# A streaming transformer step: the last output tile by token half, and the next norm and scaling beside its second half

## The chip, the cores and the metric

One core of one Trainium2 chip runs the whole step as one program. The metric is the device time of one execution, in microseconds (us); less is better.

## The reference

A two-layer trunk with a prompt of 512 tokens and a sample of 32, model width 1024. Each layer is FFN, mixer, FFN, each with a modulated norm before it and a gated, normed residual behind it:

```python
def modulated_pre(x, g, mods, j):
    return rms_norm(x, g) * (1.0 + mods[:, 3 * j + 1, None]) + mods[:, 3 * j, None]
def gated_post(x, o, g, mods, j, coef):
    return x + coef * mods[:, 3 * j + 2, None] * rms_norm(o, g)
mods = silu(c) @ ada_w[l] + ada_b[l]          # 9 x 1024 numbers for the prompt, 9 x 1024 for the sample
x = gated_post(x, swiglu(modulated_pre(x, ..., 0), w1, w3, w2), norm_post[l, 0], mods, 0, 0.5)
x = gated_post(x, mixer(modulated_pre(x, ..., 1)), norm_post[l, 1], mods, 1, 1.0)
x = gated_post(x, swiglu(modulated_pre(x, ..., 2), w1, w3, w2), norm_post[l, 2], mods, 2, 0.5)
```

The mixer is latent attention beside retention; the change doesn't touch its inside.

## The kernel before

All activations lie with features on the 128 partitions and the T = 544 tokens along the row: x is 8 tiles of 128x544 (KD = 8). TensorE (PE) multiplies in two halves of HT = 272 tokens, one PSUM bank each. Every weight and every activation is split into a high and a low part (w_hi, w_lo, h_hi, h_lo), and one product is three: hi x hi, hi x lo, lo x hi (tile3, L654). ScalarE (ACT) casts a weight chunk to w_hi (high, L1107), GpSimd (POOL) subtracts for w_lo (low, L537). There are two slots of weight chunks, so a chunk is cast only when the chunk before the last is used up (w_used), and SyncE loads the next into raw when the low part is done.

An FFN is an up phase (22 feature tiles) and an out phase of 8 output tiles with 22 k-tiles each (out_tiles, L746); the mixer's out phase has 8 k-tiles. j counts the three parts of a layer: 0 and 2 are the FFNs, 1 the mixer. During an FFN's out phase VectorE (DVE) computes the modulations (ada_group, L1443): 48 tiles with two dots each (L1454) in a layer's first FFN, 24 in its second. The dots read the conditioning vector spread over PSUM banks 4 to 7.

A "turn" is what stands between the last product of an out phase and the next stage. It is written out by hand, in the order of each engine's queue:

- After an output tile, ACT squares it (L1212) and scales it to o_buf (L1221, L1223), POOL adds the squares (L547).
- PE waits until the squares are added and, for j = 0 and 2, until all dots are done (ada_done, L772), since it now uses banks 4 and 5. It sums the squares of each token (token_sums, L675, L678), ACT takes the root (L1125), DVE the inverse (L1482), PE spreads it over the partitions (spread, L682, L686, L687).
- DVE turns over (L1477): for each of the 8 tiles o times the inverse (L1491), then x plus that (L1494); three of the eight adds go to POOL (add_odd, L556). ACT scales each new x tile to h_hi (L1136), DVE makes h_lo (L1523).
- PE's first_tiles (L690) does the first two weight chunks (w = 0, 1) in a special order: first all products with h_hi (L701, L703), each k-tile as it comes, for both chunks and both halves; then chunk 0 with h_lo (L711), and after each of its k-tiles the sum of the squares of that x tile over the partitions (pre_sum, L718, L671), which ACT makes in two buffers in turn (L1144); then chunk 1 with h_lo. ACT's root (L1121) and DVE's inverse (L1527) of these sums are needed only to read out the finished tiles.
- The third weight chunk is cast when chunk 0 is used up (w_used at its last h_lo product).

There are five such turns, after (layer 0, j = 0), (0, 1), (0, 2), (1, 0) and (1, 1), and after (1, 2) only the x update and the stores of y. At the start, (0, 0) has first_tiles without a turn before it.

## Time and profile before

| | |
|---|---|
| median of 3 runs | 2378.63 us (2377.84 to 2381.17) |
| profiled execution | 2378.93 us |
| its span | 2377.1 us |
| granted TensorE clock, mean | 0.98 |
| PE, DVE, ACT, POOL busy | 97%, 52%, 34%, 37% |

### The profile page before, as it was taken

To read this page: it belongs to the slowest core of one execution; us is meant where nothing else is said; L and a number is where in the kernel's file an instruction comes from. 1 tells how busy PE (TensorE), PEld (TensorE's weight loads), DVE (VectorE), ACT (ScalarE), POOL (GpSimd) and SP (SyncE) were. 2 spreads that over 40 slices of the span, in tenths; PEclk is the share of its full clock that TensorE was granted. 3 is DMA by queue.
4 is the path that set the end of the run, shared out by engine and by line. 5 is a ranking of instruction groups with operands and counts; after the bars stand their busy time and mean duration, and the time that the engine had idled before them with its cause. 6 is when DMAs were issued, how large, how long until landed. Compare 5 with 4: busy or idle time off the path is not lost.

```text
span 2377.1 us, 44378 instructions
## 1 busy us (share of the span) xinstructions
PE 2311.3 (97%) x17736; PEld 2195.5 (92%) x17736; DVE 1234.7 (52%) x2091; ACT 808.5 (34%) x1332; POOL 878.9 (37%) x382
## 2 busy tenths in 40 slices
PE   8999999999999999999999999999999999999997
PEld 7999999899558999999999999998994699999997
DVE  5333379867471433338143333996856524333561
ACT  3322232333454423332243333224343543333321
POOL 1333444334113344434434434443431153333353
PEclk8999999999999999999999999999999999999999
DMA  6222268322211122236312223782231022222552
GB/s 232 89 88 88 83 236 295 141 89 80 73 36 54 63 84 84 88 129 241 107 60 84 88 88 121 272 271 100 80 111 51 1 71 71 88 88 88 190 200 73
DMA packets 73240, 272.05 MB, mean 114 GB/s; under 512 B 8960, under 2 KB 10368, under 8 KB 72640
## 3 DMA queue, kind: packets, MB, share of 16 engines
q1 hardware_dynamic: 73152, 270.84, 33.1%
q8 instruction: 60, 0.98, 0.2%
q14 instruction: 28, 0.23, 0.0%
HBM read 267.36 MB, written 3.45 MB: 114 GB/s over the span
## 4 chain that ended last, share of the span: by engine, by line
PE 70%; issue 16%; DVE 6%; POOL 3%; DMA 2%; ACT 2%; SPq 1%; DVEq 0%; POOLq 0%; ACTq 0%
PE ps L661 19%; PE ps L665 19%; PE ps L662 19%; POOL w_lo L540 3%; DVE wide_v L1454 2%; PE ps L671 2%; DMA ada_w<-in_ada 2%; PE ps L701 1%; PE ps L703 1%; PE ps L1025 1%; PE ps L910 1%; PE ps L1048 1%; PE ps L992 1%; PE ps L998 1%; DMA ada_first<-in_ada 1%
## 5 line engine op out<-in xcount | busy, mean ns | idle before, releaser
L540 POOL TENSOR_TENSOR w_lo<-raw,w_hi 128x1024 fp32r<-128x1024 f32 (+1 forms) x304 | 785.6, 2584 | 1349.9 <-ACT w_hi L1118 956.9
L661 PE MATMUL ps<-h_hi,w_hi 128*128 128x272 f32 x3296 | 887.4, 289 | 7.7 <-POOL w_lo L540 7.7
L662 PE MATMUL ps<-h_lo,w_hi 128*128 128x272 f32 x3296 | 889.2, 287 | 0.0
L665 PE MATMUL ps<-h_hi,w_lo 128*128 128x272 f32 x3296 | 685.7, 289 | 0.0
L661 PEld LDWEIGHTS ps<-h_hi,w_hi 128*128 128x128 f32 x3296 | 619.1, 188 | 10.5 <-POOL w_lo L540 10.3
L662 PEld LDWEIGHTS ps<-h_lo,w_hi 128*128 128x128 f32 x3296 | 620.9, 188 | 0.2
L1118 ACT CAST w_hi<-raw 128x1024 fp32r<-128x1024 f32 (+1 forms) x236 | 268.6, 1138 | 837.1 <-PE ps L665 753.1
L665 PEld LDWEIGHTS ps<-h_hi,w_lo 128*128 128x128 f32 x3296 | 519.2, 188 | 0.0
L661 PE MATMUL ps<-u_hi,w_hi 128*128 128x272 f32 x1408 | 381.2, 288 | 3.8 <-POOL w_lo L540 3.8
L662 PE MATMUL ps<-u_lo,w_hi 128*128 128x272 f32 x1408 | 380.2, 288 | 0.0
L1454 DVE CUSTOM_DVE_ANT_0 wide_v<-ada_w,ps 128x1024 bf16<-128x1024 f32 x288 | 332.2, 1218 | 47.5 <-DMA ada_w<-in_ada 29.4
L1541 DVE TENSOR_TENSOR wide_v<-ps,rinv 128x544 f32<-128x544 f32 x88 | 63.7, 724 | 439.5 <-PE ps L665 439.5
L665 PE MATMUL ps<-u_hi,w_lo 128*128 128x272 f32 x1408 | 292.0, 288 | 0.0
L661 PEld LDWEIGHTS ps<-u_hi,w_hi 128*128 128x128 f32 x1408 | 265.3, 188 | 4.7 <-POOL w_lo L540 4.7
L662 PEld LDWEIGHTS ps<-u_lo,w_hi 128*128 128x128 f32 x1408 | 264.8, 188 | 0.0
L1546 DVE SCALAR_TENSOR_TENSOR wide_v<-wide_v,wide_s 128x512 f32<-128x512 f32 (+1 forms) x176 | 193.9, 1140 | 104.7 <-ACT wide_s L1184 104.7
L665 PEld LDWEIGHTS ps<-u_hi,w_lo 128*128 128x128 f32 x1408 | 220.0, 188 | 0.0
L1187 ACT CAST u_hi<-wide_v 128x544 f32 (+1 forms) x88 | 56.9, 647 | 213.7 <-DVE wide_v L1546 213.7
L1111 ACT CAST w_hi<-raw 128x1024 fp32r<-128x1024 f32 x68 | 71.0, 1044 | 138.6 <-PE ps L665 88.2
L1482 DVE RECIPROCAL tok_inv<-tok_root 128x5 f32<-128x5 f32 x6 | 1.1, 189 | 205.2 <-ACT tok_root L1125 205.2
L1551 DVE TENSOR_TENSOR u_lo<-wide_v,u_hi 128x544 f32 x88 | 63.9, 726 | 80.0 <-ACT u_hi L1187 80.0
L1184 ACT ACTIVATE wide_s<-wide_s 128x512 f32<-128x512 f32 (+1 forms) x176 | 81.9, 513 | 5.6 <-DVE wide_s L1538 5.6
(256 smaller groups left out, 2382.3 us busy)
## 6 DMA issues: line engine op xcount, KB each, us to landing
raw<-in_w_up SPq DMA_DIRECT2D x176, 512.0 KB, 3.4
ada_w<-in_ada SPq DMA_DIRECT2D x144, 512.0 KB, 5.0
raw<-in_w_dn SPq DMA_DIRECT2D x64, 704.0 KB, 5.3
raw<-in_w_mix SPq DMA_DIRECT2D x64, 512.0 KB, 3.5
ada_first<-in_ada SPq DMA_DIRECT2D x10, 512.0 KB, 8.0
decay<-in_decay SPq DMA_DIRECT2D x2, 2048.0 KB, 9.8
ada_first<-in_ada_first SPq DMA_DIRECT2D x6, 512.0 KB, 11.4
x<-in_x SPq DMA_DIRECT2D x4, 544.0 KB, 16.4
```

The lines of the kernel that those rows point to most:

```text
L540: pool.tensor_tensor(w_lo[:, slot, 0:width], raw[:, slot, 0:width], w_hi[:, slot, 0:width].bitcast(F32), ALU.subtract).then_inc(lo_done.se ...
L661: pe.matmul(ps[:, bank + t, 0:width[t]], wh, hi[:, n], start=start, stop=False)
L662: pe.matmul(ps[:, bank + t, 0:width[t]], wh, lo[:, n], start=False, stop=False)
L665: last = pe.matmul(ps[:, bank + t, 0:width[t]], wl, hi[:, n], start=False, stop=stop)
L1111: nc.scalar.copy(w_hi[:, slot, 0:width], raw[:, slot, 0:width]).then_inc(hi_done.sem, 1)
L1118: nc.scalar.copy(w_hi[:, k, 0:width], raw[:, k, 0:width]).then_inc(hi_done.sem, 1)
L1184: nc.scalar.activation(wide_s[:, f, at], wide_s[:, f, at], ACT.Silu, bias=wide_s[:, f, T + 2 * v:T + 2 * v + 1]).then_inc(up_silu.sem, 1)
L1187: nc.scalar.copy(u_hi[:, bass.ds(i * 2 + f, 1), :].rearrange("p a n -> p (a n)"), tmp_v[:, f, :]).then_inc(up_hi.sem, 1)
L1454: v_.tensor_tensor_reduce(junk[v], ada_w[:, t, :], c_psum(v), 1.0, 0.0, ALU.mult, ALU.add, acc[:, v, t:t + 1]).then_inc(ada_done.sem, 1)
L1541: v_.tensor_tensor(halves(tmp_v[:, f, :]), pair(4 * f + 2), halves(rinv[:, :]), ALU.mult)
L1546: v_.scalar_tensor_tensor(out=wide_v[:, f, at], in0=wide_v[:, f, at], scalar=wide_v[:, f, T + 2 * v:T + 2 * v + 1], in1=wide_s[:, f, at], ...
L1551: v_.tensor_tensor(u_lo[:, at, :].rearrange("p a n -> p (a n)"), tmp_v[:, f, :], u_hi[:, at, :].rearrange("p a n -> p (a n)").bitcast(F32) ...
```

## The change

- The last output tile goes by token half (last_tile on PE and ACT): all its k-tiles for tokens 0 to 271, then all again for 272 to 543. Inside the second half, after four k-tiles, PE makes the first half's token sums (half_sums, with the wait for all dots), and after eleven the spread; the mixer's tile has only eight k-tiles and spreads behind the last.
- DVE updates x by half, each with 8 multiplications and 8 additions of 272 columns, all on DVE. Its inverse for the second half stands before the seventh tile of the first half.
- ACT scales x to h_hi by half (one instruction for the first half, two for the second, which ends with the 32 sample tokens).
- The second half's token sums and spread stand in first_tiles, which now goes chunk 0 with h_hi of the first half, chunk 1 with the same, then both with the second half; then the h_lo pass as before.
- ACT squares the x tiles between the second half's scalings. Tiles 0 to 3 are added by POOL (add_x_squares) and summed by PE once (early_sum); tiles 4 to 7 are summed by PE one by one, after every second k-tile of chunk 0.
- DVE's h_lo comes behind all x updates, first half first.
- In the last layer's second FFN the last 16 modulation tiles, whose results nothing used, aren't loaded or computed.

The diff cut to its core; removed lines are in the functions above.

```diff
...
+TOK_AT = [0, P, HT - P]
 TOK = len(TOK_AT)
...
+SUM_AT = HT + NS
+N_EARLY = 4
...
                 for t in range(ADA_RING, per - ahead):
                     ada_tile(0, t)
+                last = s == 1 and l == DEPTH - 1
                 with sp.Fori(1, 4 - s) as i:
...
+                    down(i, ada=not last)
                 if s == 1:
...
+            def add_x_squares(l, j, m):
+                pool.wait_ge(x_sq.sem, x_sq.at(l, j * KD + m + 1))
+                if m == 1:
+                    pool.tensor_tensor(squares[:, :], tmp_s[:, 0, :], tmp_s[:, 1, :], ALU.add).then_inc(sq_added.sem, 2)
+                else:
+                    pool.wait_ge(sq_added.sem, sq_added.at(l, j * SQ + m))
+                    pool.tensor_tensor(squares[:, :], squares[:, :], tmp_s[:, m % 2, :], ALU.add)\
+                        .then_inc(sq_added.sem, 1)
...
+                for m in range(1, N_EARLY):
+                    add_x_squares(l, j, m)
...
+            def half_sums(l, j, t):
+                if t == 0:
+                    pe.wait_ge(sq_added.sem, sq_added.at(l, (j + 1) * SQ))
+                    if j != 1:
+                        pe.wait_ge(ada_done.sem, ada_done.at(
+                            l, 2 * (ADA_A if j == 0 else ADA_A + (ADA_B if l < DEPTH - 1 else KD))))
+                token_sums(squares[:, :], t, True, False)
+                if t:
+                    pe.wait_ge(out_sq.sem, out_sq.at(l, (j + 1) * KD))
+                else:
+                    pe.wait_ge(half_sq.sem, half_sq.at(l, j + 1))
+                token_sums(tmp_s[:, 1, :], t, False, True).then_inc(sums.sem, 1)
+            def spread(l, j, t):
+                pe.wait_ge(inverted.sem, inverted.at(l, 3 * j + 2 + t))
+                for b in range(2):
+                    c = t * TOK + b
+                    pe.transpose(ps[:, 4 + t, b * P:(b + 1) * P], tok_inv[:, c:c + 1].to_broadcast([P, P]), ident[:, :])
+                c = t * TOK + 2
+                pe.transpose(ps[:, 4 + t, HT - NS:HT], tok_inv[P - NS:P, c:c + 1].to_broadcast([NS, P]),
                              ident[P - NS:P, P - NS:P]).then_inc(inv_spread.sem, 1)
...
             def first_tiles(l, j, chunk):
+                post = (l, j - 1) if j else (l - 1, 2)
                 if (l, j) == (0, 0):
                     first_high(chunk)
+                for w in range(2 if l or j else 0):
+                    pe.wait_ge(lo_done.sem, lo_done.at(l, chunk + w + 1))
+                    for k in range(KD):
+                        if w == 0 and k == 2:
+                            half_sums(*post, 1)
+                        if w == 0 and k == 5:
+                            spread(*post, 1)
+                        if w == 0:
+                            pe.wait_ge(h_high.sem, h_high.at(l, high_count(l, j, 0, k)))
+                        pe.matmul(ps[:, 2 * w, 0:HT], w_hi[:, w, k * P:(k + 1) * P], h_hi[:, k, 0:HT],
+                                  start=k == 0, stop=False)
+                        pe.matmul(ps[:, 2 * w, 0:HT], w_lo[:, w, k * P:(k + 1) * P], h_hi[:, k, 0:HT],
+                                  start=False, stop=False)
                 for k in range(KD if l or j else 0):
...
+                    pe.wait_ge(h_high.sem, h_high.at(l, high_count(l, j, 1, k)))
                     for w in range(2):
...
+                        pe.matmul(ps[:, 2 * w + 1, 0:HB], w_hi[:, w, k * P:(k + 1) * P], h_hi[:, k, HT:HT + HB],
+                                  start=k == 0, stop=False)
+                        pe.matmul(ps[:, 2 * w + 1, 0:HB], w_lo[:, w, k * P:(k + 1) * P], h_hi[:, k, HT:HT + HB],
+                                  start=False, stop=False)
                 for w in range(2):
                     for k in range(KD):
                         if w == 0:
...
+                            pe.wait_ge(h_ready.sem, h_ready.at(l, H_AT[j] + 12 + 2 * k))
                         for t, w_t in enumerate((HT, HB)):
                             n = slice(t * HT, t * HT + w_t)
                             last = pe.matmul(ps[:, 2 * w + t, 0:w_t], w_hi[:, w, k * P:(k + 1) * P], h_lo[:, k, n],
                                              start=False, stop=k == KD - 1)
...
+                        if w == 0 and k % 2:
+                            if k == KD - 1:
+                                last.then_inc(w_used.sem, 1)
+                            pre_sum(l, j, 4 + k // 2)
+                    if w == 0:
+                        early_sum(l, j)
+                last.then_inc(w_used.sem, 1)
             def pre_sum(l, j, m):
                 if not (l or j):
                     pe.wait_ge(c_kept.sem, 2)
                 pe.wait_ge(x_sq.sem, x_sq.at(l, j * KD + m + 1))
...
+                add_squares(tmp_s[:, m % 2, :], 6, m == N_EARLY, False, ones).then_inc(sums.sem, 1)
+            def early_sum(l, j):
+                pe.wait_ge(sq_added.sem, sq_added.at(l, j * SQ + N_EARLY))
+                add_squares(squares[:, :], 6, False, True, ones).then_inc(sums.sem, 1)
...
                     tile(i * 2 + 1, 1, False)
...
+                tile(KD - 2, 0, False)
+                last_tile(l, j, chunk0, per_tile, chunk_tiles, operand)
+            def last_tile(l, j, chunk0, per_tile, chunk_tiles, operand):
+                pe.wait_ge(out_ev.sem, out_ev.at(l, j * KD + KD - 2))
+                n0 = chunk0 + (KD - 1) * per_tile
+                last_k = per_tile * chunk_tiles - 1
+                for t in range(2):
+                    n = slice(t * HT, (t + 1) * HT)
+                    for q in range(per_tile):
+                        if t == 0:
+                            pe.wait_ge(lo_done.sem, lo_done.at(l, n0 + q + 1))
+                        for kk in range(chunk_tiles):
+                            k = q * chunk_tiles + kk
+                            if t and k == 4:
+                                half_sums(l, j, 0)
+                            if t and k == 11:
+                                spread(l, j, 0)
+                            hi, lo = operand(k)
+                            slot = (n0 + q) % 2
+                            wh, wl = (w[:, slot, kk * P:(kk + 1) * P] for w in (w_hi, w_lo))
+                            pe.matmul(ps[:, 2 + t, 0:HT], wh, hi[:, n], start=k == 0, stop=False)
+                            pe.matmul(ps[:, 2 + t, 0:HT], wh, lo[:, n], start=False, stop=False)
+                            last = pe.matmul(ps[:, 2 + t, 0:HT], wl, hi[:, n], start=False, stop=k == last_k)
+                        if t:
+                            last.then_inc(w_used.sem, 1)
+                    if t == 0:
+                        last.then_inc(half_mm.sem, 1)
+                if last_k < 11:
+                    spread(l, j, 0)
+                if l == DEPTH - 1 and j == 2:
+                    half_sums(l, j, 1)
+                    spread(l, j, 1)
...
+            def scaled(l, j, t, m):
+                if l or j:
+                    act.wait_ge(x_new.sem, x_new.at(l, x_count(j - 1, t, m)))
+                elif t == 0:
+                    act.wait_ge(x_in[m // 2].sem, 16)
+                for v, n in ((0, slice(HT, NP_)), (1, slice(NP_, T))) if t else ((0, slice(0, HT)),):
+                    nc.scalar.activation(h_hi[:, m, n], x[:, m, n], ACT.Copy, scale=mul_pre[:, j, v, m:m + 1])\
+                        .then_inc(h_high.sem, 1)
...
+            def last_tile(l, j, chunk0, per_tile, o_buf, pre):
+                in_u = per_tile == 2
+                ahead = 3 if in_u else 0
+                if pre is not None:
+                    pre_l, pre_j, chunk = pre
+                act.wait_ge(half_mm.sem, half_mm.at(l, j + 1))
+                act.wait_ge(sq_added.sem, sq_added.at(l, j * SQ + N_EARLY + KD - 2))
+                nc.scalar.activation(tmp_s[:, 1, 0:HT], ps[:, 2, 0:HT], ACT.Square).then_inc(half_sq.sem, 1)
+                act.wait_ge(columns.sem, columns.at(l, (6, COL_A, COL_A + 6)[j]))
+                nc.scalar.activation(o_buf[:, KD - 1, 0:HT], ps[:, 2, 0:HT], ACT.Copy,
+                                     scale=mul_post[:, j, 0, KD - 1:KD]).then_inc(half_ev.sem, 1)
+                act.wait_ge(sums.sem, sums.at(l, (j + 1) * SUMS - 1))
+                token_root(0)
+                if pre is not None:
+                    high(pre_l, chunk, 0, KD * P)
+                    if in_u:
+                        shift_columns(pre_l, pre_j)
+                        for m in range(ahead):
+                            scaled(pre_l, pre_j, 0, m)
+                act.wait_ge(w_used.sem, w_used.at(l, chunk0 + KD * per_tile))
+                nc.scalar.activation(tmp_s[:, 1, HT:T], ps[:, 3, 0:HT], ACT.Square).then_inc(out_sq.sem, 1)
+                if pre is not None:
+                    high(pre_l, chunk + 1, 1, KD * P)
+                    if not in_u:
+                        shift_columns(pre_l, pre_j)
+                    for m in range(ahead, ahead + 2):
+                        scaled(pre_l, pre_j, 0, m)
+                act.wait_ge(sums.sem, sums.at(l, (j + 1) * SUMS))
+                token_root(1)
+                n = NP_ - HT
+                nc.scalar.activation(o_buf[:, KD - 1, HT:NP_], ps[:, 3, 0:n], ACT.Copy,
+                                     scale=mul_post[:, j, 0, KD - 1:KD])
+                nc.scalar.activation(o_buf[:, KD - 1, NP_:T], ps[:, 3, n:HT], ACT.Copy,
+                                     scale=mul_post[:, j, 1, KD - 1:KD]).then_inc(out_ev.sem, 1)
+                if pre is not None:
+                    for m in range(ahead + 2, KD):
+                        scaled(pre_l, pre_j, 0, m)
+                    pre_scale(pre_l, pre_j, chunk)
             def pre_scale(l, j, next_chunk):
...
                 def squared(m):
                     if m < 2:
                         act.wait_ge(sums.sem, sums.at(l, j * SUMS))
+                    elif m < N_EARLY + 2:
+                        act.wait_ge(sq_added.sem, sq_added.at(l, j * SQ + max(2, m - 1)))
                     else:
...
+                        act.wait_ge(sums.sem, sums.at(l, j * SUMS + m - N_EARLY - 1))
...
                 if l or j:
...
                     for m in range(KD):
...
+                        scaled(l, j, 1, m)
+                        if m >= 3:
+                            squared(m - 3)
+                    for m in range(KD - 3, KD):
...
+                    def invert(t):
+                        dve.wait_ge(rooted.sem, rooted.at(l, 3 * j + 2 + t))
+                        n = slice(t * TOK, (t + 1) * TOK)
+                        v_.reciprocal(tok_inv[:, n], tok_root[:, n]).then_inc(inverted.sem, 1)
+                    invert(0)
+                    for t in range(2):
+                        n = slice(t * HT, (t + 1) * HT)
+                        dve.wait_ge(inv_spread.sem, inv_spread.at(l, 2 * j + t + 1))
+                        for m in range(KD):
+                            if t == 0 and m == KD - 2:
+                                invert(1)
+                            if t == 0 and m == KD - 1:
+                                dve.wait_ge(half_ev.sem, half_ev.at(l, j + 1))
+                            else:
+                                dve.wait_ge(out_ev.sem, out_ev.at(l, j * KD + m + 1))
+                            c = x_count(j, t, m)
+                            prod = ps[:, 6 + m % 2, 0:HT]
+                            if t or m >= 2:
+                                dve.wait_ge(x_new.sem, x_new.at(l, c - 2))
+                            v_.tensor_tensor(prod, o_buf[:, m, n], ps[:, 4 + t, 0:HT], ALU.mult).then_inc(x_prod.sem, 1)
+                            dve.wait_ge(x_prod.sem, x_prod.at(l, c))
+                            v_.tensor_tensor(x[:, m, n], x[:, m, n], prod, ALU.add).then_inc(x_new.sem, 1)
...
+                            if first and t == 0 and m % 2 == 0:
+                                dve.wait_ge(x_in[m // 2].sem, 16)
+                            dve.wait_ge(h_high.sem, h_high.at(l, high_count(l, j, t, m)))
+                            for v, n in ((0, slice(HT, NP_)), (1, slice(NP_, T))) if t else ((0, slice(0, HT)),):
+                                v_.scalar_tensor_tensor(out=h_lo[:, m, n], in0=x[:, m, n], scalar=mul_pre[:, j, v, m:m + 1],
+                                                        in1=h_hi[:, m, n].bitcast(F32), op0=ALU.mult, op1=ALU.subtract)\
+                                    .then_inc(h_ready.sem, 1)
...
```

## Rows read from the trace of the kernel before

**Rows 1.** The page's part 1: busy time, share of the span and instructions of each engine.
```profile
PE 2311.3 (97%) x17736; PEld 2195.5 (92%) x17736; DVE 1234.7 (52%) x2091; ACT 808.5 (34%) x1332; POOL 878.9 (37%) x382
```
**Rows 2.** Windows, the five turns and the end: length, busy time (instructions), clock, DMA.
```profile
443.80:475.60 31.80, 26.09 (x155) 23.88 (x154) 22.34 (x45) 17.33 (x35) 10.31 (x6) 0.84 0.21 73
777.80:806.80 29.00, 25.16 (x154) 23.15 (x153) 17.88 (x33) 17.31 (x35) 8.78 (x5) 0.88 0.12 37
1195.00:1223.70 28.70, 24.86 (x155) 22.86 (x153) 17.93 (x33) 17.36 (x35) 8.81 (x5) 0.88 0.06 19
1611.80:1643.60 31.80, 26.19 (x154) 23.93 (x153) 22.65 (x45) 17.27 (x35) 10.86 (x6) 0.84 0.20 73
1944.40:1973.70 29.30, 25.50 (x154) 23.51 (x152) 17.83 (x33) 17.38 (x35) 8.78 (x5) 0.88 0.12 37
2361.50:2377.10 15.60, 2.94 (x25) 2.58 (x24) 9.24 (x14) 1.80 (x5) 4.00 (x3) 0.65 0.37 143
```
**Rows 3.** PE's wait for the dots: timeline (start, length), then waits (total, times, longest).
```profile
445.62 0.58 PE L678 MATMUL ps<-ones,squares 128*128 128x1 f32 x4 [1.79 <-DVE acc L1454]
...
PE ps L678 <- DVE acc L1454: 3.6, 2, 1.8
```
**Rows 4.** DVE's timeline, last dot of the first turn.
```profile
444.24 1.22 DVE L1454 CUSTOM_DVE_ANT_0 wide_v<-ada_w,ps 128x1024 bf16<-128x1024 f32 x1
445.38 0.08 DVE L1454 DVE_READ_ACCUMULATOR2_ANT acc<- 128x1 f32 x1
```
**Rows 5.** PE's timeline, third turn.
```profile
1194.23 0.29 PE L662 MATMUL ps<-u_lo,w_hi 128*128 128x272 f32 x1
...
1194.61 0.42 PE L665 MATMUL ps<-u_hi,w_lo 128*128 128x272 f32 x2
1194.86 1.17 PE L678 MATMUL ps<-ones,squares 128*128 128x1 f32 x10
...
1197.73 0.65 PE L686 MATMUL ps<-ident,tok_inv 128*128 128x128 f32 x4 [0.58 <-DVE tok_inv L1482]
...
1201.14 0.56 PE L701 MATMUL ps<-h_hi,w_hi 128*128 128x272 f32 x1 [2.59 <-issue]
...
1223.65 0.39 PE L661 MATMUL ps<-h_hi,w_hi 128*128 128x272 f32 x1 [0.67 <-POOL w_lo L540]
```
**Rows 6.** DVE's timeline, third turn.
```profile
1198.59 0.73 DVE L1491 TENSOR_TENSOR ps<-o_ffn,ps 128x544 f32<-128x544 f32 x1 [0.91 <-PE ps L687]
1199.35 0.72 DVE L1494 TENSOR_TENSOR x<-x,ps 128x544 f32<-128x544 f32 x1
1199.99 0.71 DVE L1491 TENSOR_TENSOR wide_v<-o_ffn,ps 128x544 f32<-128x544 f32 x1
...
1208.34 6.69 DVE L1523 SCALAR_TENSOR_TENSOR h_lo<-x,mul_pre,h_hi 128x512 fp32r<-128x512 f32 x16
```
**Rows 7.** The chain that ended last, first turn: start, length, what.
```profile
456.83 0.23 PE ps L701
...
468.46 0.92 PE ps L671 x4
```
**Rows 8.** POOL's timeline, last tile before the third turn (its products start at 1178.4).
```profile
1179.87 3.23 POOL L540 TENSOR_TENSOR w_lo<-raw,w_hi 128x1408 fp32r<-128x1408 f32 x1 [5.09 <-ACT w_hi L1118]
1183.05 1.35 POOL L547 TENSOR_TENSOR squares<-squares,wide_s 128x544 f32<-128x544 f32 x1
```
**Rows 9.** POOL beside DVE, timeline; then groups by shape: count, busy us, mean ns, idle.
```profile
1261.37 2.40 POOL L540 TENSOR_TENSOR w_lo<-raw,w_hi 128x1024 fp32r<-128x1024 f32 x1 [3.56 <-ACT w_hi L1118]
1262.25 2.22 DVE L1546 SCALAR_TENSOR_TENSOR wide_v<-wide_v,wide_s 128x512 f32<-128x512 f32 x2 [1.22 <-ACT wide_s L1184]
...
L1546 DVE SCALAR_TENSOR_TENSOR wide_v<-wide_v,wide_s 128x512 f32<-128x512 f32 x88 | 179.6, 2041 | 104.7 <-ACT wide_s L1184 104.7
L1523 DVE SCALAR_TENSOR_TENSOR h_lo<-x,mul_pre,h_hi 128x512 fp32r<-128x512 f32 x48 | 35.8, 745 | 0.0
L1523 DVE SCALAR_TENSOR_TENSOR h_lo<-x,mul_pre,h_hi 128x32 fp32r<-128x32 f32 x48 | 11.8, 245 | 0.0
```

223 lines of the change are left out of this document (75 added, 148 removed).

## The prediction

> **What bounds the kernel now.** I read the page first: TensorE (PE) is busy for 97% of the span, DVE (VectorE) for 52% [rows 1]. So a change elsewhere is worth only what it gives PE back. Then I measured the places where PE isn't fed, the five turns from the last product of one out phase to the first product of the next stage's second pair of tiles [rows 2]: 31.8, 29.0, 28.7, 31.8 and 29.3 us, 150.6 in all, and 15.6 us after the very last product. One turn's own PE work is small: 96 products at 0.126 us (three of them in 0.38 [rows 5]; 12.1 us) and eight square sums at 0.92 (7.4) [rows 7], with 2.3 of token sums on top [rows 5]. Some 7 to 10 us per turn are to be had.
>
> Where do they go? In the third turn (end of products at 1195.0) the token sums take 2.3 us, then come root, inverse and spread, and PE waits for the first scaled tile until 1201.14 [rows 5]; DVE starts the x updates at 1198.59, ends them at about 1208.2 and has h_lo ready at 1215.0 [rows 6]. PE restarts at the low clock (0.23 us a product, in the first turn still so at 456.83, four microseconds after its restart [rows 7]) and ends the turn with a 0.67 us wait for the low part of the third weight chunk [rows 5]. In the two FFN-to-mixer turns (first and fourth) PE also waits 1.8 us for DVE's last modulation dots before it may use banks 4 to 7 [rows 3, 4]: this is why these two are 3 us longer.
>
> **The change, part by part.** Times below are from the old end of the last product (E) and made against the profiled execution's 2378.9 us (span 2377.1; the runs' median, 2378.6, differs by nothing that matters). The engines' orders are taken from the diff and each instruction is put behind its engine and its waits.
>
> (1) The last tile goes by halves. An FFN tile has 132 products, 16.6 us, so its first half ends at E-8.3. Its second chunk's low part is needed after 33 products (4.2 us) instead of 66; in the third turn GpSimd (POOL) delivers it 4.7 us after the tile's start [rows 8]: 0.6 us of new wait, 2.1 in the first turn.
>
> (2) Token sums and spread of the first half stand between the second half's products: 6 sums at 0.23 (ten records in 1.17 us [rows 5]) and 3 transposes at 0.16, 1.9 us of PE, then the same again in the next tile. The products now end at E+2.6 (0.6+1.4+0.5, rounded). For that, DVE can start x at E-1.6 instead of E+3.6.
>
> (3) half_sums(0) keeps the wait for all modulation dots, and it now stands at the fifth k-tile of the second half, with 54 products queued behind it. In the first turn the dots end at E+1.6 and PE gets through at E+1.8 [rows 3, 4]; the change moves none of this (DVE is at its dots back to back, 1.14 us each [rows 4]). PE will be there at E-6 (E-5 with the 2.1 us above). So it stands 6 to 8 us in place of 1.8, and the 54 products (6.8 us), which used to be done, come after it. They restart at the low clock, some 20 of them at 0.23: +2.0. The tile ends at E+12.5 (1.8+1.4+6.8+2.0+0.5). The queue behind is PE's alone; DVE, ScalarE (ACT) and POOL are through with theirs.
>
> (4) DVE's x updates become 32 instructions of 272 instead of 13 of 544 (three adds leave POOL). A pair costs 1.40 us at 544 [rows 6]; the part by column is 1.04 ns (745 ns for 512 columns and 245 for 32 of one instruction [rows 9]), so 272 columns less take off 0.28 twice: 0.84 a pair, 13.4 us for 16 against 9.7 now. Six pairs run from E-1.6 to E+3.5; then DVE's inverse of the second half waits for sums that PE makes after the first two k-tiles of the next product (done E+3.8; ACT has a weight cast and scaled tiles ahead of the root, so the inverse stands at E+5.2). The other ten pairs end at E+13.7, against E+13.2 now: the early start is spent. The Trainium skill (VectorE: DVE Perf Modes, the section on the TRN2 errata) says the same against this change, that each instruction pays a fixed cost and tiles of 512 or more are wanted; its table would make a 272-column instruction with a PSUM source 0.41 us where I get 0.44, some 1 us less per turn and 5 in the sum, but for 544 it gives 0.69 where the trace has 0.73, so I keep the rows.
>
> (5) h_lo comes after all of x. Today's 16 instructions take 6.69 us [rows 6], 0.83 a tile; without 272 of the columns that is 0.55 for the second half's two, and 0.42 for the first half's one. PE's pass with h_lo waits for the second half's tiles, and DVE makes all eight of the first half before them: the first is ready 4.1 us after x (0.2+3.4+0.5), E+17.8, the last 3.9 us later.
>
> (6) POOL now adds three pairs of squares, 1.35 us each [rows 8], at just that time, and here the trace has a price: DVE's h_lo instruction reads two SBUF tensors, as L1546 does, and L1546 at 512 columns takes 2.04 us on average with POOL's subtraction running where L1523 takes 0.745; one started at 1262.25 and ended half a us after POOL's instruction that ran till 1263.77 [rows 9]. So each POOL add holds h_lo up for its length: 0 to 4.1 us a turn; two of the three fall behind the end of x, I take 2.8. First h_lo pair at E+20.6, the last at E+24.4.
>
> (7) PE then has 16 products, five sums instead of eight (three less are 2.8 us, the purpose of the POOL part), and 16 products: 2.0+4.6+2.0, with 0.6 of waits for h_lo, to E+29.9. The third chunk's low part is ready before that, as w_used now comes two sums and 16 products ahead; the 0.67 us wait goes.
>
> So a turn like the third takes 29.9 against 28.7: **+1.2**. The mixer's turns (second, fifth): the last tile has 48 products, only 12 of them after half_sums, so the spread stands behind the products and DVE starts x at E+2.1; the same chain gives 32.1 against 29.0 and 29.3: **+3.1 and +2.8**. First and fourth: 12.5-2.6 us later than the third, 39.7 against 31.8: **+7.9 each**. The end of the program: x of the first half is hidden, the second half's last add ends at E+12.9 against 13.2, **-0.3**. The very first turn has three sums less, but its fifth square waits behind two POOL adds: **0** (between -1 and +1). The modulation tiles dropped from the last layer (16 loads, 32 dots at 1.14 us) stand beside PE's products and bound nothing: 0. The sum is +22.6: 2401.5.
>
> (8) The clock. In each turn PE is idle and then at the low clock for its first products [rows 2, 7], and the mean granted clock over a turn is 0.84 to 0.88 [rows 2]. With the change PE has a second hole, from about E+15 to E+20.6 with only single k-tiles in the 6 us before it. If the clock falls again there, the h_lo pass starts low: 0.88 of 28.7 us is 3.4 us of clock gone or 6.9 us at the lower of the two levels (1.2 and 2.4 GHz), of which 5.4 under load would lose 2.7. Bounds 0 and 5.4 a turn; I take it in half of the five turns, +6.5. **2408.**
>
> **Rivals.** (B) The clock falls in every turn and stays for double that time: 2401.5+13.5 to +27, 2415 to 2428. (C) POOL's adds don't hold up h_lo, since they fall beside x, whose instructions read one operand from PSUM and keep 0.72 us in this turn [rows 6], where POOL adds as well: 14 us less, 2388. Against it: the squares come one per scaled tile, late. (D) The dots end earlier than PE's arrival, so (3) costs nothing: 9.8 us less twice, 2382, no change. Nothing in the diff makes the dots of the first FFN of a layer faster, and the trace has two waits of this kind, 3.6 us together [rows 3]. (E) The other side, faster: DVE's chain is short enough for PE to be fed, which decides once its ten late pairs and nine tiles of h_lo fit between E+5.2 and E+12.6, when PE is through with the products without h_lo: 0.4 us each in place of 0.84 and 0.42 to 0.55. A turn is then PE's own work, 12.1+4.6+2.8+1.0 = 20.5 us, and 29.7 with the stall of (3): 2.1 less twice, 8.5, 8.2 and 8.8 less: 2349. The Trainium skill (Perfetto Trace Analysis, Optimizing Scalar/DVE Operations) supports it: where a vector engine isn't saturated but leaves bubbles elsewhere, smaller instructions finish work sooner. Within the turn DVE isn't far from that: busy for 17.9 of 28.7 us now [rows 2], and by (4) to (6) at work or held from E-1.6 to E+24.4.
>
> **Chances.** Forecast (2395 to 2415) 0.55, B 0.18, C 0.12, D 0.07, E 0.08. Faster by over 0.2% (4.8 us, about what a measurement of this kernel can tell): 0.08; within: 0.07; slower: 0.85. The range 2385 to 2424 leaves out D, E and B's far end, 0.18.
>
> **What would show it.** In the new trace: PE's token sums of the first half preceded by an idle of 6 us or more, released by a DVE dot, in two turns; the last product some 12 us after the last dot there; 16 pairs of x updates 0.84 us apart; single h_lo instructions of over 1 us beside POOL's three adds; five turns of 39.7, 32.1, 29.9, 39.7, 32.1 us plus clock; 0.5 in the granted clock at the h_lo pass. I am wrong if the dots end before PE arrives, if pairs are nearer 0.6 us, or if h_lo runs at 0.42 us throughout.

## The result, and the profile after

The changed kernel takes 2414.4 us (median of 4 runs, 2413.6 to 2415.6) against 2379.9 us for the kernel before (4 runs beside them, 2377.8 to 2381.7): a ratio of 1.0146, 95% interval 1.0128 to 1.0163, slower by 34.5 us. The forecast was 2408.0 with a range of 2385 to 2424, slower.

The profiled execution has a span of 2411.8 us (before 2377.1), a mean granted clock of 0.97, and this first part of its page (engine, busy us, share, instructions):

```profile
PE 2321.2 (96%) x17694; PEld 2196.7 (91%) x17694; DVE 1235.9 (51%) x2177; ACT 820.5 (34%) x1392; POOL 878.5 (36%) x382
```

As in [rows 1], TensorE (PE) is the bound, with 10 us more of busy time though it has 42 instructions fewer: its work takes longer, and the mean clock is lower (0.97 for 0.98). The windows that answer to [rows 2] say where. They run from the old end of the last product (E: the last tile's start plus the time that its products need) to the next stage's second pair of tiles; columns: from:to, length, then busy us and instructions of PE, its weight loads, DVE, ACT and POOL, the granted clock, and two DMA columns.

```profile
443.80:485.80 42.00, 33.98 (x200) 30.63 (x201) 27.72 (x73) 19.21 (x43) 11.25 (x6) 0.82 0.15 55
787.70:822.80 35.10, 27.98 (x146) 24.54 (x146) 24.73 (x61) 18.65 (x43) 11.15 (x6) 0.76 0.11 31
1210.40:1242.50 32.10, 26.97 (x155) 23.30 (x154) 23.25 (x57) 17.25 (x39) 10.61 (x6) 0.84 0.12 33
1630.10:1673.10 43.00, 36.30 (x200) 32.72 (x201) 27.36 (x73) 19.21 (x43) 11.25 (x6) 0.77 0.15 54
1975.20:2008.70 33.50, 25.58 (x147) 22.85 (x146) 24.82 (x61) 18.62 (x43) 11.17 (x6) 0.85 0.11 32
2396.40:2411.80 15.40, 4.80 (x38) 4.42 (x37) 11.63 (x30) 1.19 (x4) 0.00 (x0) 0.75 0.38 145
```

The five turns take 185.7 us where they took 150.6: +35.1, the whole loss (the span is 34.7 longer). The first and fourth lost 10.2 and 11.2, the second, third and fifth 6.1, 3.4 and 4.2; the end of the program gained 0.2. DVE is busy for 5 to 7 us more in each turn. PE's waits in the whole execution (what waited, for what: us in total, times, longest) name the places:

```profile
PE ps L680 <- DVE acc L1556: 15.7, 2, 8.1
PE ps L739 <- DVE h_lo L1636: 13.2, 5, 2.9
PE ps L729 <- ACT h_hi L1197: 9.1, 11, 1.4
PE ps L663 <- POOL w_lo L540: 7.7, 8, 1.2
...
PE ps L722 <- POOL w_lo L540: 3.5, 2, 1.8
```

The first line answers to [rows 3]: the wait of the token sums for DVE's dots was 3.6 us in two turns and is 15.7. In PE's timeline of the first turn (start, length, what, and in brackets the idle time before it and what ended it) it stands inside the last output tile:

```profile
437.73 0.29 PE L828 MATMUL ps<-u_hi,w_lo 128*128 128x272 f32 x1
446.09 1.41 PE L680 MATMUL ps<-ones,squares 128*128 128x1 f32 x6 [8.08 <-DVE acc L1556]
...
448.64 0.57 PE L826 MATMUL ps<-u_hi,w_hi 128*128 128x272 f32 x1
449.01 0.43 PE L827 MATMUL ps<-u_lo,w_hi 128*128 128x272 f32 x1
```

DVE's last dot ended at 445.86 + 0.08, no earlier after E than in [rows 4]. PE stood still for 8.08 us with 54 products of the tile queued behind the wait, and did the first 13 of them at 0.23 us a product (0.43 a record) in place of 0.126.

The third turn has no such wait. DVE there, which answers to [rows 6] (E is 1210.4):

```profile
1209.02 0.45 DVE L1604 TENSOR_TENSOR ps<-o_ffn,ps 128x272 f32<-128x272 f32 x1 [2.65 <-PE ps L705]
1209.50 0.44 DVE L1606 TENSOR_TENSOR x<-x,ps 128x272 f32<-128x272 f32 x1
1209.86 0.44 DVE L1604 TENSOR_TENSOR ps<-o_ffn,ps 128x272 f32<-128x272 f32 x1
...
1215.70 0.18 DVE L1586 RECIPROCAL tok_inv<-tok_root 128x3 f32<-128x3 f32 x1 [1.61 <-ACT tok_root L1187]
...
1223.72 0.44 DVE L1606 TENSOR_TENSOR x<-x,ps 128x272 f32<-128x272 f32 x1
1224.07 0.81 DVE L1616 TENSOR_TENSOR h_lo<-mods,h_hi 128x16 fp32r<-128x16 f32 x2
1224.80 9.90 DVE L1636 SCALAR_TENSOR_TENSOR h_lo<-x,mul_pre,h_hi 128x272 fp32r<-128x272 f32 x24
```

A pair of x updates takes 0.84 us (1209.02 to 1209.86), the x chain starts before E and still ends at E+13.7, and h_lo takes 9.90 us. Beside it POOL adds squares, and PE waits (POOL's and PE's timelines, the same turn):

```profile
1223.42 1.34 POOL L557 TENSOR_TENSOR squares<-wide_s 128x544 f32<-128x544 f32 x1 [6.29 <-ACT wide_s L1257]
1225.53 2.89 POOL L560 TENSOR_TENSOR squares<-squares,wide_s 128x544 f32<-128x544 f32 x2 [0.77 <-ACT wide_s L1257]
```

```profile
1226.11 0.40 PE L729 MATMUL ps<-h_hi,w_hi 128*128 128x276 f32 x1 [1.40 <-ACT h_hi L1197]
...
1227.25 0.60 PE L729 MATMUL ps<-h_hi,w_hi 128*128 128x276 f32 x1 [0.26 <-ACT h_hi L1197]
...
1230.96 1.37 PE L739 MATMUL ps<-h_lo,w_hi 128*128 128x272 f32 x4 [2.43 <-DVE h_lo L1636]
...
1240.31 2.37 PE L739 MATMUL ps<-h_lo,w_hi 128*128 128x272 f32 x16
1242.52 0.30 PE L663 MATMUL ps<-h_hi,w_hi 128*128 128x272 f32 x1
```

This is the second hole: single k-tiles from 1222.8 on, with an idle of 1.40 us between two of them, then 2.43 us of idle ahead of 1230.96. Two windows, before and behind 1226.6, give the granted clock (third column from the right) as 1.00 and 0.50:

```profile
1208.40:1226.60 18.20, 15.76 (x113) 13.98 (x111) 15.42 (x38) 14.06 (x35) 7.20 (x4) 1.00 0.20 59
1226.60:1236.80 10.20, 7.52 (x24) 5.89 (x23) 8.11 (x22) 2.46 (x6) 1.68 (x2) 0.50 0.00 0
```

So it fell behind the single k-tiles, ahead of the longer idle, stayed low for 10.2 us, and the h_lo pass starts at half speed, four products in 1.37 us. The first of the two windows shows what the early start did buy: in this turn the hole behind the last tile is closed and the clock no longer falls there, where in the kernel before it was low for 6.8 us of the turn. In the other four turns it falls in both holes. The 1.40 us are POOL's too: ACT's next square needs the buffer that POOL's add frees at 1224.76, and the scaled tile stands behind that square (with short adds, in tiny_adds below, the idle there is 0.37 us). The next tile starts without a wait, where [rows 5] had 0.67 us.

### The profile page after: what moved, and what is told of

Its sections match the earlier page's. It is cut to its first block, busy times and chain, and to the rows that moved or that the text cites. A ratio compares the mean times of both kernels' runs of the same rounds, so it can differ in the third digit from the quotient of the medians.

```text
span 2411.8 us, 44344 instructions
## 1 busy us (share of the span) xinstructions
PE 2321.2 (96%) x17694; PEld 2196.7 (91%) x17694; DVE 1235.9 (51%) x2177; ACT 820.5 (34%) x1392; POOL 878.5 (36%) x382
## 4 chain that ended last, share of the span: by engine, by line
PE 67%; issue 16%; DVE 8%; POOL 3%; ACT 2%; DMA 2%; SPq 1%; DVEq 0%; POOLq 0%; ACTq 0%
PE ps L667 18%; PE ps L663 18%; PE ps L664 18%; POOL w_lo L540 3%; DVE wide_v L1556 2%; DMA ada_w<-in_ada 1%; PE ps L673 1%; DVE h_lo L1636 1%; DVE ps L1604 1%; PE ps L739 1%; PE ps L1086 1%; PE ps L826 1%; PE ps L971 1%; DMA x<-in_x 1%; PE ps L828 1%
## 5 line engine op out<-in xcount | busy, mean ns | idle before, releaser
L663 PE MATMUL ps<-u_hi,w_hi 128*128 128x272 f32 x1232 | 332.7, 288 | 3.9 <-POOL w_lo L540 3.9
L664 PE MATMUL ps<-u_lo,w_hi 128*128 128x272 f32 x1232 | 332.5, 289 | 0.0
L1556 DVE CUSTOM_DVE_ANT_0 wide_v<-ada_w,ps 128x1024 bf16<-128x1024 f32 x256 | 295.1, 1217 | 32.8 <-DMA ada_w<-in_ada 15.9
L667 PE MATMUL ps<-u_hi,w_lo 128*128 128x272 f32 x1232 | 255.3, 288 | 0.0
L663 PEld LDWEIGHTS ps<-u_hi,w_hi 128*128 128x128 f32 x1232 | 231.8, 188 | 4.7 <-POOL w_lo L540 4.7
L664 PEld LDWEIGHTS ps<-u_lo,w_hi 128*128 128x128 f32 x1232 | 232.2, 188 | 0.0
L667 PEld LDWEIGHTS ps<-u_hi,w_lo 128*128 128x128 f32 x1232 | 192.8, 188 | 0.0
```

Source lines behind the costliest of these rows:

```text
L663: pe.matmul(ps[:, bank + t, 0:width[t]], wh, hi[:, n], start=start, stop=False)
L664: pe.matmul(ps[:, bank + t, 0:width[t]], wh, lo[:, n], start=False, stop=False)
L667: last = pe.matmul(ps[:, bank + t, 0:width[t]], wl, hi[:, n], start=False, stop=stop)
L1556: v_.tensor_tensor_reduce(junk[v], ada_w[:, t, :], c_psum(v), 1.0, 0.0, ALU.mult, ALU.add, acc[:, v, t:t + 1]).then_inc(ada_done.sem, 1)
```

## The experiments

Each is compared with runs of the kernel before on the same chip (medians of 2379.8 to 2380.5 us). Distances below are taken against the medians, 2414.4 for the changed kernel.

| kernel | us | ratio to before (95%) |
|---|---|---|
| changed kernel | 2414.4 | 1.0146 (1.0128 to 1.0163) |
| late_half_sums | 2404.6 | 1.0107 (1.0090 to 1.0124) |
| filled_hole | 2404.2 | 1.0099 (1.0082 to 1.0116) |
| late_and_filled | 2393.8 | 1.0059 (1.0042 to 1.0075) |
| low_by_half | 2409.2 | 1.0118 (1.0101 to 1.0135) |
| late_and_low_by_half | 2393.4 | 1.0054 (1.0037 to 1.0070) |
| squares_on_pe | 2413.3 | 1.0146 (1.0129 to 1.0163) |
| tiny_adds | 2397.0 | 1.0072 (1.0056 to 1.0089) |
| late_low_tiny_adds | 2376.4 | 0.9984 (0.9974 to 0.9994) |
| narrow_alone | 2381.3 | 1.0005 (0.9995 to 1.0014) |
| squares_alone | 2373.2 | 0.9971 (0.9960 to 0.9981) |
| squares_and_early_sums | 2372.8 | 0.9973 (0.9962 to 0.9984) |
| dropped_tiles | 2380.0 | 0.9998 (0.9989 to 1.0008) |

**late_half_sums: the token sums behind the last product.** In the first FFN of each layer, so in the first and fourth turn only:

```diff
-                            if t and k == 4:
+                            if t and k == 4 and j:
                                 half_sums(l, j, 0)
-                            if t and k == 11:
+                            if t and k == 11 and j:
                                 spread(l, j, 0)
...
-                if last_k < 11:
+                if j == 0:
+                    half_sums(l, j, 0)
+                if last_k < 11 or j == 0:
                     spread(l, j, 0)
```

> The changed kernel, but in the two FFN-to-mixer turns (j = 0) the first half's token sums and spread stand behind the last product instead of inside the second half, so that the wait for the dots holds back no product. Theory (the misplaced wait costs): PE's idle of 8.4 and 7.9 us inside the tile shrinks to under 1 us behind it, DVE starts x at about E+4.5 instead of E+9.6 and E+10.0 (E is the old end of the last product), both turns get 5.3 us shorter, from 42.1 and 43.0 to about 37, and the kernel takes 2404, ratio to before 1.010. Rival (DVE's long chain and the clock set the turn whatever PE does before): the turns stay over 41 us and the kernel is at 2412 or more.

2404.6: 9.9 us less, as the theory had it. PE's timeline of its first turn (E 444.15):

```profile
446.12 0.80 PE L680 MATMUL ps<-ones,squares 128*128 128x1 f32 x6 [1.00 <-DVE acc L1558]
...
451.30 0.60 PE L722 MATMUL ps<-h_hi,w_hi 128*128 128x272 f32 x1 [2.55 <-POOL w_lo L540]
```

The wait for the dots is down to 1.00 us; the last product now starts at E+0.7 where it was at E+13.6. Of these 12.9 us the turn gives back 5.2 only (next tile at E+36.9 against E+42.1; 6.2 in the fourth turn): what is late next is DVE's chain, and beside it stands a wait that no step of the prediction named, 2.55 us for the low part of the first weight chunk. ACT casts that chunk behind the root of the first half's token sums, and POOL's 2.4 us for w_lo come after the cast.

**filled_hole: dummy products in the second hole.** After the k-tiles of the second scaled half PE does products that nothing reads, 36 in each turn:

```diff
                     for w in range(2):
                         pe.matmul(ps[:, 2 * w + 1, 0:HB], w_hi[:, w, k * P:(k + 1) * P], h_hi[:, k, HT:HT + HB],
                                   start=k == 0, stop=False)
                         pe.matmul(ps[:, 2 * w + 1, 0:HB], w_lo[:, w, k * P:(k + 1) * P], h_hi[:, k, HT:HT + HB],
                                   start=False, stop=False)
+                    for i in range(4 if 3 <= k < KD - 1 else 20 if k == KD - 1 else 0):
+                        pe.matmul(ps[:, 4, HT:512], w_hi[:, 0, 0:P], h_hi[:, 0, 0:512 - HT], start=True, stop=True)
```

> The changed kernel with idle products added on PE (240 columns into an unused part of bank 4, results not read) after the k-tiles 3 to 7 of the second half's h_hi pass, 4 each and 20 at the end, to keep PE at work where it had 1.7 to 3.2 us of idle. Theory (the second fall of the clock costs 1.4 to 3.3 us a turn, 12 in all): the granted clock stays at 1 from there to the end of the turn, and the kernel takes 2402 to 2406. Rival (the slow stretch is no cost, since DVE's chain is late anyway): 2414 or more, by the added products.

2404.2: 10.2 us less, inside the theory's 2402 to 2406, with more work on PE and nothing taken from any other engine. The third turn's window and PE's timeline in it (E 1205.4):

```profile
1205.40:1235.00 29.60, 27.34 (x191) 24.89 (x191) 23.29 (x57) 17.21 (x39) 10.61 (x6) 1.00 0.12 37
...
1222.82 2.40 PE L734 MATMUL ps<-h_hi,w_hi 128*128 128x240 f32 x20
1225.94 1.06 PE L741 MATMUL ps<-h_lo,w_hi 128*128 128x272 f32 x4 [0.72 <-DVE h_lo L1638]
```

The h_lo pass starts at the same E+20.5 as in the changed kernel, but at a granted clock of 1.00, and the turn takes 29.6 us, not 32.1. In this trace the second fall is gone from all five turns; the first one lasts 3.4 us longer than in the changed kernel's trace in the fourth and fifth, so 10.2 us is what the second fall costs net of that. 29.6 is also within 0.3 of the 29.9 that the prediction's sum had for this turn without the clock.

**late_and_filled: both cures.**

> late_half_sums and filled_hole together (dummy products of TensorE between the half tiles of the second scaled half, token sums of FFN's out phases behind the last product). If the two costs are separate, 2414.4 - 9.9 - 10.2 = 2394.3 (2392 to 2397). If both cures work against the same fall of the clock, they overlap: 2398 to 2404. The distance to late_and_low_by_half tells what 16 real products in the hole give beyond their effect on the clock.

2393.8: 20.6 us less, and 9.9 and 10.2 make 20.1. The two costs are separate.

**low_by_half: the h_lo products by half as well.** PE does the first half's 16 as soon as its h_lo is there, in the hole:

```diff
+                for w in range(2):
+                    for k in range(KD):
+                        if w == 0:
+                            pe.wait_ge(h_ready.sem, h_ready.at(l, H_AT[j] + k + (3 if l or j else 1)))
+                        pe.matmul(ps[:, 2 * w, 0:HT], w_hi[:, w, k * P:(k + 1) * P], h_lo[:, k, 0:HT],
+                                  start=False, stop=k == KD - 1)
                 for w in range(2):
...
-                        for t, w_t in enumerate((HT, HB)):
-                            n = slice(t * HT, t * HT + w_t)
-                            last = pe.matmul(ps[:, 2 * w + t, 0:w_t], w_hi[:, w, k * P:(k + 1) * P], h_lo[:, k, n],
-                                             start=False, stop=k == KD - 1)
+                        last = pe.matmul(ps[:, 2 * w + 1, 0:HB], w_hi[:, w, k * P:(k + 1) * P], h_lo[:, k, HT:HT + HB],
+                                         start=False, stop=k == KD - 1)
```

> The changed kernel with one thing different: the products of h_lo (TensorE, 32 per turn) also go by token half, 16 of the first half for both features, and then 16 of the second half with the five sums among them. The first half's h_lo is ready from 14.4 us after the last product on, in the hole that stood before this pass (20.5 us in the third turn), so 16 products fill it. Theory (the second hole is an order of TensorE's work and costs the clock): the gain is that of the dummy products, 10.2 us, and up to 1.5 us a turn more for products that have left the tail: 2397 to 2404. Rival 1: 16 short products keep the clock no more than 16 of nothing, it falls as before, and only the 1 to 2 us of moved products count: 2406 to 2410. Rival 2: the tail is set by the h_lo of the second half and the low part of the third chunk, not by TensorE: under 1 us a turn: 2410 to 2415.

2409.2: 5.2 us less, the time that rival 1 gave. PE's timeline of the third turn (E 1208.9):

```profile
1227.29 4.06 PE L737 MATMUL ps<-h_lo,w_hi 128*128 128x272 f32 x13 [0.38 <-DVE h_lo L1640]
...
1240.10 0.40 PE L663 MATMUL ps<-h_hi,w_hi 128*128 128x272 f32 x1 [0.73 <-POOL w_lo L540]
```

The hole is filled (an idle of 0.38 us in place of 2.43), but 13 of the 16 products, in 4.06 us, are at half speed: they come when the clock has just fallen, at E+18.4, behind the single k-tiles. It falls in every turn, as that rival said, but not for as long: 27.2 us in the five second falls of this trace, against 40.8 in the changed kernel's. And with a shorter tail the next tile waits for the third chunk's low part, 0.73 us, the wait that the kernel before had.

**late_and_low_by_half: this and the late sums.**

> Both cures: the first half's token sums and spread of the FFN's out phases stand behind the last product (as in late_half_sums, 9.9 us in two turns), and the h_lo products go by half (as in low_by_half). Theory (two separate costs): the gains add up, 2414.4 - 9.9 - (10 to 17) = 2387 to 2394, so still 0.3 to 0.6% above the kernel before: what is left is the chain of DVE (32 half-width updates, 24 h_lo instructions, POOL's hold), which the halves have made longer. Rival: with the waits gone the early start of the first half pays, and the kernel is level with the one before or faster: under 2380. Rival on the other side: one fall of the clock only moves to another place, and the two gains overlap: 2397 to 2404.

2393.4: 21.0 us less than the changed kernel, more than the parts' 9.9 + 5.2. The other 5.9 us go with the clock: in the third turn it is low for 3.4 us here and for 6.8 in low_by_half, and in the second and fifth the second fall of 3.4 us is missing. The late sums don't touch these turns, and no run holds the clock fixed here, so the 5.9 us aren't shown to be the clock's alone, and how long a fall lasts hangs on more than the order within a turn; what it hangs on these runs don't show. The kernel stays 13 us above the one before.

**squares_on_pe: no adds on POOL.** All eight square sums of x are done by PE again, the rest of the change stays:

```diff
-N_EARLY = 4
+N_EARLY = 0
...
-                        if w == 0 and k % 2:
+                        if w == 0:
...
-                            pre_sum(l, j, 4 + k // 2)
-                    if w == 0:
-                        early_sum(l, j)
+                            pre_sum(l, j, k)
```

> The changed kernel with all eight square sums on PE as before the change, none added on GpSimd. Theory (GpSimd's adds hold back DVE's h_lo): no h_lo instruction over 0.6 us, the first h_lo product 2.2 to 2.6 us earlier in each turn, and the three more sums (2.8 us) and the wait for the third weight chunk (0.7 us) use that up again: 2414 to 2420 in all. Rival (the hold costs nothing on the path): the h_lo pass starts when it does now and each of the six turns is longer by 3.5 us, 2435.

2413.3 (2411.9 to 2417.9), not to be told from the changed kernel (2413.6 to 2415.6) and just under the theory's 2414 to 2420. DVE's timeline, third turn:

```profile
1223.09 7.72 DVE L1632 SCALAR_TENSOR_TENSOR h_lo<-x,mul_pre,h_hi 128x272 fp32r<-128x272 f32 x24
```

24 instructions in 7.72 us, against 9.90 with POOL's adds beside them (and 0.55 more for the shift columns ahead of them: 0.81 against 0.26). The last h_lo of this turn comes 2.75 us earlier after E, where the prediction took 2.8 for the hold; the three more sums on PE eat what it gives.

**tiny_adds: POOL's adds at 2 columns of 544.** What the adds cost by their length, with no work put on PE. The kernel leaves the squares of tiles 0 to 3 out of the sum but for two columns:

```diff
-                    pool.tensor_tensor(squares[:, :], tmp_s[:, 0, :], tmp_s[:, 1, :], ALU.add).then_inc(sq_added.sem, 2)
+                    if not (l or j):
+                        pool.memset(squares[:, 2:T], 0.0)
+                    pool.tensor_tensor(squares[:, 0:2], tmp_s[:, 0, 0:2], tmp_s[:, 1, 0:2], ALU.add).then_inc(sq_added.sem, 2)
...
-                    pool.tensor_tensor(squares[:, :], squares[:, :], tmp_s[:, m % 2, :], ALU.add)\
+                    pool.tensor_tensor(squares[:, 0:2], squares[:, 0:2], tmp_s[:, m % 2, 0:2], ALU.add)\
```

> The changed kernel, with POOL's three adds of x squares done on 2 columns of 544 (the rest of the four early squares is left out of the sum; a memset stands before the first of them once). All waits and counts stay, so what goes is the time in which POOL's adds hold up DVE's x updates and h_lo. In squares_on_pe the last h_lo of the third turn came 2.75 us earlier than in the changed kernel (21.53 against 24.28 after the last product), and some of it is clock. Theory (the hold lies on the chain that ends the turn, also through the hole and the clock): 2.2 to 2.8 us a turn, 11 to 14 in five: 2400 to 2403. Rival 1: the hole is shorter by 2.8 and the second clock fall shortens or goes with it: under 2398. Rival 2 (the tail is TensorE's own work, h_lo is early enough without): under 1 us a turn, 2409 to 2414.

2397.0: 17.4 us less, more than five times 2.75 (13.8), so rival 1. The third turn's window:

```profile
1204.60:1231.40 26.80, 23.76 (x154) 20.73 (x154) 20.48 (x57) 16.98 (x39) 7.32 (x6) 1.00 0.11 40
```

With h_lo 2.75 us earlier the clock doesn't fall a second time in this turn (1.00), and 26.8 us is less than the 28.7 of the kernel before. The two costs can be read apart here: filled_hole's 29.6 us for this turn also stands at a clock of 1.00, so POOL's adds cost 2.8 us of the turn and the clock the 2.5 from 32.1 to 29.6. In the other four turns it falls a second time for 3.4 us, where in the changed kernel it fell for 6.8, 10.2, 10.2 and 3.4. And squares_on_pe, in which h_lo is as early as here, takes 16.3 us more: that is the price of three more sums a turn on PE, behind h_lo.

**late_low_tiny_adds: no stall, no hold.**

> late_and_low_by_half, with POOL's three adds of x squares done on 2 columns (as in tiny_adds; the sum of squares is left incomplete). Both stalls of TensorE's order are gone there, and 13 us remain above the kernel before. Theory (what remains is DVE's chain, of which POOL's hold is 2.75 us in each of five turns): 11 to 14 us less, 2380 to 2383, level with the kernel before. Rival: the chain's other parts (DVE takes over three x sums from POOL, the inverse of the second half in the middle of the x updates, narrow instructions) or TensorE's sums behind it are the bound, and the hold is hidden for the most part: 2388 to 2393.

2376.4, 4.1 us under the kernel before, and 17.0 less than late_and_low_by_half, more than the theory's 11 to 14 and below its 2380 to 2383: that hold costs more than its length, as in tiny_adds. No kernel with the halves was faster here, and this one leaves the squares of four of eight x tiles out of the sum. Added up on PE they would be three sums of 0.92 us in each of the five turns, 13.8 us, or the 16.3 between squares_on_pe and tiny_adds: 2390 to 2393, an estimate.

**narrow_alone: the kernel before with narrow DVE instructions.**

```diff
-                        v_.tensor_tensor(prod, o_buf[:, m, :], along(4), ALU.mult).then_inc(x_prod.sem, 1)
+                        for n in (slice(0, HT), slice(HT, T)):
+                            made = v_.tensor_tensor(prod[:, n], o_buf[:, m, n], along(4)[:, n], ALU.mult)
+                        made.then_inc(x_prod.sem, 1)
...
-                        for v, n in enumerate(GROUPS):
...
+                        for v, n in ((0, slice(0, HT)), (0, slice(HT, NP_)), (1, slice(NP_, T))):
```

> The kernel before with DVE's instructions alone made narrow: each x product and x sum is written in two instructions of 272 columns, and the first 512 columns of each h_lo tile in two (272 and 240); nothing starts earlier, nothing waits for a half, POOL keeps its three sums. A product or sum costs 0.84 for two where it cost 0.72: with five tiles of two on DVE and three of one, the x chain is 13 x 0.12 = 1.6 us longer per turn. Theory (DVE's chain through x holds TensorE's first pass in the kernel before, so narrow instructions are a cost of their own in the change): 1 to 1.6 us a turn and again at the end of the program, 6 to 10 us: 2386 to 2390. Rival: TensorE at the low clock sets that pass (its first products are slower than the scaled tiles come), so the longer chain is hidden: within 2 us of the kernel before, 2380 to 2382.

2381.3, 1.5 us above before with an interval that has 1 in it: the rival, not the theory. Two halves of a product take 0.79 us against the 0.73 of [rows 6] (a first start to the second's end):

```profile
1201.70 0.79 DVE L1492 TENSOR_TENSOR ps<-o_ffn,ps 128x272 f32<-128x272 f32 x2 [0.91 <-PE ps L687]
```

x and h_lo end 0.4 and 1.5 us later after E in the third turn, and the next tile starts only 0.4 us later. Written as two products and then two sums, narrow instructions cost little, and in this kernel PE doesn't wait for what they cost: 0.82 us from one pair of halves to the next for 0.76. In the changed kernel each sum comes right behind its own product, 0.47 us after it (1209.02 to 1209.50), and the next product 0.36 after the sum: 0.84 for half a tile, 1.66 a tile against 1.40. Its x chain is 15.1 us against 9.7, by 32 x 0.42 = 13.4 for 13 x 0.72 = 9.4, of which 2.2 to 2.5 are the three sums that POOL used to do, and by the 1.6 us idle ahead of the second inverse at 1215.70.

**squares_alone: the kernel before with only the squares' part** (POOL adds tiles 0 to 3, ACT squares between its scalings, PE does five sums):

```diff
+            def add_x_squares(l, j, m):
...
+                for m in range(1, N_EARLY):
+                    add_x_squares(l, j, m)
...
-                        if w == 0:
-                            pre_sum(l, j, k)
+                        if w == 0 and k % 2:
...
+                            pre_sum(l, j, 4 + k // 2)
+                    if w == 0:
+                        early_sum(l, j)
```

> The kernel before with one part of the change alone: squares of x tiles 0 to 3 added on GpSimd, squares of tiles made between the scalings, four sums and one on PE. Theory: PE saves three sums (2.8 us) and the 0.67 us wait for the third chunk in each of six first_tiles, but the fourth and later squares wait for GpSimd's adds and h_lo is held up to 4 us, of which DVE's lead over PE hides most: 1 to 3 us gained a turn, 2365 to 2374, ratio 0.994 to 0.998. Rival (the hold is on the path here too): within 2 us of before.

2373.2: 0.3% faster than the kernel before, with an interval clear of 1, at the near end of the theory's range. DVE and POOL in its third turn:

```profile
1205.55 1.86 DVE L1520 TENSOR_TENSOR x<-x,wide_v 128x544 f32<-128x544 f32 x1
...
1207.50 8.88 DVE L1549 SCALAR_TENSOR_TENSOR h_lo<-x,mul_pre,h_hi 128x512 fp32r<-128x512 f32 x16
```

```profile
1205.47 1.36 POOL L563 TENSOR_TENSOR squares<-wide_s 128x544 f32<-128x544 f32 x1 [0.78 <-ACT wide_s L1166]
1207.60 3.79 POOL L566 TENSOR_TENSOR squares<-squares,wide_s 128x544 f32<-128x544 f32 x2 [0.77 <-ACT wide_s L1166]
```

The hold is here too: h_lo takes 8.88 us for 6.69, the last x sum, which reads two SBUF tensors, 1.86 for 0.72, and POOL's two adds 1.86 and 1.78 for 1.36, since they wait for DVE as well. But PE is still busy with h_hi products while this goes on, and it saves 2.8 us a turn behind them. The net is 0.5 to 1.2 us in the three turns without dots (the next tile 28.2 to 28.3 us after the last product, for 28.8 to 29.5), under the theory's 1 to 3. In each of these three turns the clock is low for 10.2 us in this trace and was for 6.8 in that of the kernel before; how much of the difference to 2.8 us is that, no run shows.

**squares_and_early_sums: this, with the token sums in another bank**, so that they needn't wait for the dots:

```diff
-            return ps[:, bank + 1, SUM_AT:SUM_AT + TOK]
+            return ps[:, 1, SUM_AT:SUM_AT + TOK]
...
-                if j != 1:
-                    pe.wait_ge(ada_done.sem, ada_done.at(l, 2 * (ADA_A if j == 0 else ADA_A + ADA_B)))
+                pe.wait_ge(out_ev.sem, out_ev.at(l, j * KD + KD - 1))
                 token_sums(squares[:, :], 4, True, False)
...
+                if j != 1:
+                    pe.wait_ge(ada_done.sem, ada_done.at(l, 2 * (ADA_A if j == 0 else ADA_A + ADA_B)))
                 spread(l, j, 4)
```

> squares_alone with TensorE's token sums put in bank 1, which the last but one output tile has left, so that they no longer wait for DVE's modulation dots (1.8 us in the first and the fourth turn); the wait for the dots moves to the spread, which writes banks 4 and 5. Theory A (that wait is on the path): two turns 1.8 us shorter, 2373.2 - 3.6 = 2369.6. Theory B (it isn't: DVE itself stands between its last dot and the inverse with the columns it makes of the dots, until 448.4 in the first turn of the kernel before, and the inverse starts right behind them): the same as squares_alone within 1 us, 2372 to 2374.

2372.8, the same as squares_alone: theory B. PE and DVE in the first turn:

```profile
444.17 1.17 PE L691 MATMUL ps<-ones,squares 128*128 128x1 f32 x10
...
449.36 1.09 PE L699 MATMUL ps<-ident,tok_inv 128*128 128x128 f32 x4 [2.88 <-DVE tok_inv L1509]
```

```profile
446.30 2.23 DVE L1486 TENSOR_TENSOR mods<-acc,ada_b 128x4 f32 x2 [0.16 <-DVE acc L1481]
...
449.03 0.18 DVE L1509 RECIPROCAL tok_inv<-tok_root 128x5 f32<-128x5 f32 x1
```

The sums start at 444.17, 2.0 us before DVE is through with its last dot at 446.14, and PE then waits for the inverse, which stands behind what DVE makes of the dots. In the kernel before the 1.8 us of [rows 3] were thus hidden behind DVE's work on the dots; the same wait moved forward by the change has nothing to hide it.

**dropped_tiles: the kernel before without the last 16 modulation tiles.**

> The kernel before with one part of the change alone: the last layer doesn't load the 16 modulation tiles that nothing reads, and DVE doesn't make their 32 dots. Theory: they stand beside TensorE's products of the last out phase and bound nothing: the same as before within 1 us (2379 to 2381). Rival: their loads or dots delay the weight chunks or the squares of that phase: 2 to 4 us faster.

2380.0, ratio 0.9998: nothing, as in the forecast.

## Why the prediction was right, and where it was too small

The direction, the places and most sizes held. By its own steps, in us after E, forecast and measured (starts of PE's and DVE's instructions in the trace of the changed kernel):

| step | forecast | measured |
|---|---|---|
| (1) wait for the second chunk's low part, first turn | 2.1 | 0.6 |
| (2) last product's end, third turn | 2.6 | 2.9 |
| (2) DVE starts x, third turn | -1.6 | -1.4 |
| (3) dots' wait lets PE through, first and fourth | 1.8 | 2.3, 1.8 |
| (3) idle ahead of it | 6 to 8 | 8.1, 7.6 |
| (3) last tile's end, first and fourth | 12.5 | 13.9, 14.3 |
| (4) a pair of x updates | 0.84 | 0.84 |
| (4) end of x, third turn | 13.7 | 13.7 |
| (4) end of x, second and fifth (13.7 and the 2.2 from 29.9 to 32.1) | 15.9 | 16.9, 16.6 |
| (6) hold by POOL's adds, third turn | 2.8 | 2.75 |
| (6) PE's h_lo pass starts, third turn | 20.6 | 20.5 |
| (6) last h_lo, third turn | 24.4 | 24.3 |
| (7) third turn without a second fall | 29.9 | 29.6 (filled_hole) |
| (8) second fall of the clock, us in all | 6.5 | 10.2 (filled_hole) |
| very first turn; end of the program; dropped tiles | 0; -0.3; 0 | +0.5; -0.2; 0 |

**Step (8), the second fall of the clock, is the term that was too small.** It was put at half of five turns, 6.5 us, so at 2.6 a turn; dummy products in the hole take off 10.2, which is five turns at 2.0. So the clock fell twice as often as forecast (in every turn, for 3.4 to 10.2 us) and each fall cost less, and that the two errors partly cancel is luck. A fall in every turn was in the text as rival B, which gave 2415 to 2428; 2414.4 lies in the forecast's own band (2395 to 2415), 0.6 us below B's near end. In the trace of before the granted clock was lowered in each of the five turns [rows 2] and no row showed a hole that kept it: "half of the turns" had no row behind it. With 10.2 for 6.5 the sum is 2411.7.

**The other 2.7 us** are in step (3) and in the turns of the mixer. In step (3) the tile ended 1.4 and 1.8 later than forecast, by a dot that ended 0.4 later in one turn and by the low clock at the token sums themselves (12 of them in 2.55 us against 0.23 a sum in the step's 1.4). In the mixer's turns x ended 1.0 and 0.7 us later than the sum has it. The second turn shows why (PE's and DVE's timelines, E 787.7):

```profile
791.34 0.36 PE L722 MATMUL ps<-h_hi,w_hi 128*128 128x272 f32 x1 [1.77 <-POOL w_lo L540]
...
795.44 0.59 PE L722 MATMUL ps<-h_hi,w_hi 128*128 128x272 f32 x1 [1.29 <-ACT h_hi L1197]
...
797.87 0.45 DVE L1604 TENSOR_TENSOR ps<-o_mix,ps 128x272 f32<-128x272 f32 x1 [1.47 <-PE ps L705]
```

The cast of the first chunk stands behind the token root, so PE gets to its first product with h_hi at E+3.7 only, a wait of the same kind as the 2.55 us in late_half_sums. Everything in PE's queue behind it is late too, the second half's sums and spread among them, and DVE stands idle for that spread between the two halves of x: 1.47 us here, 1.12 in the fifth turn. The prediction had no wait there. No run took the cast out of the way, so that it is the first cause is read from the trace and not shown. The parts don't close either: in filled_hole, without a second fall, the five turns take about 40.4, 33.1, 29.6, 41.1 and 33.4 us, 4.1 above the sum's 173.5 and not 2.7, and where the rest of the kernel gave 1.4 back stays open. Step (1) had 2.1 us for a wait of 0.6, without effect, since in that turn PE comes to the longer wait for the dots right behind it.

**Rival C** (POOL's adds cost nothing) was wrong: they cost 17.4 us (tiny_adds). By length that is 13.8, if all five turns are like the third; the rest goes with the shorter falls of the clock, and only for the third turn are the two measured apart (2.8 and 2.5). The forecast had 14 for the hold. The row that decided it, one instruction of another shape in another stage [rows 9], was enough. It also agrees with the Trainium skill (SBUF — State Buffer, 🔬 SBUF: two separate sides), by which DVE and GpSimd share a port pair that whichever instruction starts first keeps for its whole length, on DVE's side if it has two SBUF inputs: h_lo instructions of 0.49 us took 1.58 beside an add of 1.36, while the x update beside the first add (1223.72), which reads one operand from PSUM, kept its 0.44.

**Rival D** (the dots end early) was wrong, and **rival E** (PE fed throughout) too. Its condition was that ten pairs and nine tiles of h_lo fit into 7.4 us; from the second inverse at 1215.70 they took 15.2 us, until PE got the first tile of the second half at 1230.96. The rule that the prediction set beside it, of the Trainium skill (Perfetto Trace Analysis, Optimizing Scalar/DVE Operations), that smaller instructions can finish work sooner where the vector engine isn't saturated, did not hold for this order of the work. The fixed cost is a part of that: 1.66 us for 1.40 a tile, 2.1 us a turn on a chain that PE waits for (in narrow_alone, where PE doesn't wait for it, narrow instructions cost 1.5 us in all, not to be told from none). The larger part, by the trace, is the order: both halves' x come ahead of any h_lo, so that the first h_lo is no earlier than with whole tiles, E+14.4 against E+13.3. A kernel that makes the first half's h_lo ahead of the second half's x would have tested this; none was run.

What the change was worth in parts, by the runs: the squares' part alone -6.9 us; the dropped tiles 0; the misplaced wait +9.9, the second fall of the clock +10.2; and 20.6 us that are left between late_and_filled and squares_alone. This remainder is put down to the longer DVE chain by the times in the traces; POOL's hold, hidden in squares_alone and not here, is the one piece of it that a run shows.

## What to carry to other kernels

When work is moved ahead, list every wait that moves with it and ask what covered it where it was: 1.8 us that were hidden behind DVE became 8 us of an idle TensorE with 54 products queued behind them. Closing a hole early was worth nothing here, since another opened later in the same turn, and it was paid twice, in idle time and in slow products behind it. And before adding to GpSimd's queue, look at what VectorE reads at that time: here an instruction with two SBUF operands waited out the GpSimd instruction beside it, and one with a PSUM operand didn't.

## What the runs showed of the hardware

- In the third turn the granted clock stayed at 1.00 where single k-tiles came with idles of 0.37 us between them and an idle of 1.24 us behind them (tiny_adds), and fell to 0.5 for 10.2 us in the changed kernel, where one of the idles between them was 1.40 us. The fall began half a microsecond after that idle's end, ahead of the idle of 2.43 us, so it wasn't the longer wait that brought it.
- The hold works in both directions: in squares_alone POOL's adds of 1.36 us took 1.86 and 1.78 beside DVE's h_lo.
- Products that arrive just after the fall don't bring the clock back: of 16 real ones in low_by_half 13 ran at half speed, and the low clock lasted 6.8 us.
- Thirty-six dummy products of 240 columns a turn, 0.11 us each (twenty in 2.40 us), left the third turn's h_lo pass where it was, at E+20.5, and made the kernel 10.2 us shorter: work added to the busiest engine.
